# State-space stage of a hybrid decoder step: output products 128 rows wide, the state products of a pair's two groups in turn

## The reference

```python
def s5_mixer(x, ...):
    u = x.reshape(B, L, S5_GROUPS, S5_GROUP)            # 64 groups of 16 channels
    a_re, a_im = mag * cos(li * dt), mag * sin(li * dt)  # 64 complex states a group
    bu_re = einsum('blgc,gpc->blgp', u, bb_re)           # and bu_im
    h = scan(h[t] = a * h[t-1] + bu[t])                  # complex
    y = (einsum('gcp,blgp->blgc', c_re, h_re) - einsum('gcp,blgp->blgc', c_im, h_im)
         + d_skip * u)
    y = gelu(y)
    a, g = split(einsum('bld,de->ble', y, w_glu), 2)
    return a * sigmoid(g), h_re[:, -1], h_im[:, -1]
```

## Time and profile before

| | us |
|---|---|
| median of 3 runs | 1486.23 |
| lowest, highest | 1483.96, 1486.32 |
| span of the profiled execution | 1484.9 |
| PE busy in it | 1419.2 (96%) |
| weight loads (PEld) busy | 1348.5 (91%) |
| DVE busy | 687.8 (46%) |
| ACT busy | 437.6 (29%) |
| POOL busy | 367.2 (25%) |

### The profile page before, as it was taken

One profiled execution on the slowest core, in us unless ns is written; L12 is line 12 of the kernel. 1 busy time (PEld: TensorE's weight loads), 2 busy tenths in 40 slices (PEclk: granted clock), 3 DMA queues, 4 the chain that ended last, 5 costly groups with the idle time before them and its releaser, 6 DMA issues.

```text
span 1484.9 us, 26234 instructions
## 1 busy us (share of the span) xinstructions
PE 1419.2 (96%) x10503; PEld 1348.5 (91%) x10503; DVE 687.8 (46%) x902; ACT 437.6 (29%) x648; POOL 367.2 (25%) x368
## 2 busy tenths in 40 slices
PE   4999999999999999999985999999999999999997
PEld 3999977689999999999984777899999999999997
DVE  6653335656945733434438465134443343332443
ACT  4311143423422413314310011322342341331423
POOL 3010024425999700000376221012200000000032
PEclk9999989999999999999996575699999999999999
DMA  4233221114232223222378131232232222322222
GB/s 136 72 86 85 84 58 39 54 48 104 71 90 81 85 85 85 85 84 77 93 152 104 33 73 41 68 91 76 82 85 84 75 83 85 85 85 85 78 78 79
DMA packets 239142, 119.60 MB, mean 81 GB/s; under 512 B 35512, under 2 KB 235888, under 8 KB 239088
## 3 DMA queue, kind: packets, MB, share of 16 engines
q1 hardware_dynamic: 238832, 118.78, 30.5%
q10 hardware_dynamic: 256, 0.06, 0.0%
HBM read 108.08 MB, written 10.73 MB: 80 GB/s over the span
## 4 chain that ended last, share of the span: by engine, by line
PE 89%; DVE 6%; ACT 1%; issue 1%; SPq 1%; DMA 1%; POOL 0%; DVEq 0%; ACTq 0%; POOLq 0%
PE ps L309 71%; PE ps L1705 5%; PE ps L1703 3%; PE ps L1552 2%; PE ps L1525 2%; DVE wlo L293 1%; PE ps L1684 1%; PE ps L1643 1%; PE ps L1515 1%; PE ps L1561 1%; PE ps L1555 1%; DVE R L330 1%; DMA raw<-in_ffn_w_down 1%; PE ps L1578 0%; PE ps L1764 0%
## 5 line engine op out<-in xcount | busy, mean ns | idle before, releaser
L288 ACT ACTIVATE whi<-raw 128x1024 fp32r<-128x1024 f32 x177 | 187.1, 1057 | 521.9 <-PE ps L309 486.6
L309 PE MATMUL ps<-hid_hi,whi 128*128 128x288 f32 x1408 | 303.1, 296 | 10.4 <-DVE wlo L293 10.4
L309 PE MATMUL ps<-xg_hi,whi 128*128 128x288 f32 x1424 | 306.3, 296 | 3.2 <-DVE wlo L293 1.7
L309 PE MATMUL ps<-xg_hi,wlo 128*128 128x288 f32 x1424 | 304.6, 295 | 0.0
L309 PE MATMUL ps<-xg_lo,whi 128*128 128x288 f32 x1424 | 302.8, 294 | 0.0
L309 PE MATMUL ps<-hid_hi,wlo 128*128 128x288 f32 x1408 | 301.7, 295 | 0.0
L309 PE MATMUL ps<-hid_lo,whi 128*128 128x288 f32 x1408 | 300.6, 295 | 0.0
L293 DVE TENSOR_TENSOR wlo<-raw,whi 128x1024 fp32r<-128x1024 f32 x177 | 247.6, 1399 | 102.6 <-ACT whi L288 102.4
L309 PEld LDWEIGHTS ps<-hid_hi,whi 128*128 128x128 f32 x1408 | 226.4, 189 | 11.4 <-DVE wlo L293 6.3
L309 PEld LDWEIGHTS ps<-xg_hi,whi 128*128 128x128 f32 x1424 | 228.2, 188 | 5.6 <-issue 2.3
L309 PEld LDWEIGHTS ps<-xg_lo,whi 128*128 128x128 f32 x1424 | 228.4, 188 | 0.0
(11 more groups left out here) (347 smaller groups left out, 1260.8 us busy)
## 6 DMA issues: line engine op xcount, KB each, us to landing
raw<-in_ffn_w_up SPq DMA_DIRECT2D x64, 512.0 KB, 4.0
raw<-in_ffn_w_down SPq DMA_DIRECT2D x64, 512.0 KB, 4.0
raw<-in_mlstm_w_in SPq DMA_DIRECT2D x25, 512.0 KB, 3.8
raw<-in_s_w_glu SPq DMA_DIRECT2D x16, 512.0 KB, 3.9
raw<-in_mlstm_w_out SPq DMA_DIRECT2D x8, 512.0 KB, 4.0
MT<-d_taps SPq DMA_DIRECT2D x48, 64.0 KB, 2.5
d_u<-unat SPq DMA_DIRECT2D x8, 288.0 KB, 2.3
U<-d_u SPq DMA_DIRECT2D x16, 144.0 KB, 6.3
```

The costliest lines, as they stand in the source:

```text
L288: nc.scalar.activation(whi[:, s], raw[:, s], ACT.Copy).then_inc(whi_done, 1)
L309: last = nc.tensor.matmul(ps[:, 2 * s + c, 0:HN], w[:, s, k, :], a[:, k, c * HN:(c + 1) * HN], start=(k == 0 and n == 0), stop=(k == KT - ...
```

## The change

The output of a quarter's group is one accumulation of 128 partitions instead of two of 64. For each quarter the taps' products of both groups come first (weights 128 x 128 instead of 128 x 64, twice), then the state products: real part of group 0, of group 1, imaginary part of group 0, of group 1 (weights 64 x 128 instead of 64 x 64). The waits and the last instruction's signal stay.

```diff
                 for q in range(4):
+                    o = [ps[:, 6 + g2, q * COLS:(q + 1) * COLS] for g2 in range(2)]
                     for g2 in range(2):
-                        g8, st = 2 * q + g2, slice(g2 * SP, (g2 + 1) * SP)
-                        for hf in range(2):
-                            o = ps[hf * 64:(hf + 1) * 64, 6 + g2, q * COLS:(q + 1) * COLS]
-                            nc.tensor.matmul(o, taps_of[k][:, g8, hf * 64:(hf + 1) * 64], U2[:, 8 * k + g8, :], start=True, stop=False)
-                            for ri in range(2):
-                                last = nc.tensor.matmul(
-                                    o, CA[st, ri, 4 * k + q, 1 + 4 * hf:5 + 4 * hf, :].rearrange("p j c -> p (j c)"),
-                                    Hst[st, s, ri, q, 0:COLS], start=False, stop=(ri == 1))
+                        nc.tensor.matmul(o[g2], taps_of[k][:, 2 * q + g2, :], U2[:, 8 * k + 2 * q + g2, :], start=True, stop=False)
+                    for ri in range(2):
+                        for g2 in range(2):
+                            st = slice(g2 * SP, (g2 + 1) * SP)
+                            last = nc.tensor.matmul(o[g2], CA[st, ri, 4 * k + q, 1:T + 1, :].rearrange("p j c -> p (j c)"),
+                                                    Hst[st, s, ri, q, 0:COLS], start=False, stop=(ri == 1))
                 last.then_inc(sy_done, 1)
```

## The result

The changed kernel takes a median of 1433.28 us (1429.04 to 1435.41, 4 runs) beside 1486.28 (1483.96 to 1489.10, 4 runs) for the kernel before: ratio 0.963, 95% interval 0.9605 to 0.9654. It is faster and inside the range, by 53 us where 65 were forecast. The profiled execution took 1433.83 us, its span 1431.5.

A forecast was written before the change was run, and what follows sets the result against it. PE's answers were taken as the bound. 69.3 us saved on PE, less 3 of waiting and one in the tail, left 65; the 1484.9 us span became 1419.9, and 1.3 outside it made 1421 us, range 1410 to 1442.

The forecast's parts named there:

- my own case: The prediction's main case for the whole kernel: 1421 us, with its own range 1412 to 1428; chance 0.68.
- sign for paced weights: In the answers' trace: records 0.2 us apart or more would show the forecast wrong, with weights setting the pace.
- What bounds the kernel: In the stage, PE's answers are the bound: eight calls take 120.3 us, 15.04 each, with PE busy throughout.
- New price: A step of the changed answers on PE: 6.4 us at 1.2 GHz, 3.6 at 2.4, middle of the bounds.
- the rival on wide weights: In the answers, 128x128 weights pace records at 0.24 us each at 1.2 GHz: 32 us saved, 1454; chance 0.07.
- The loop after it: PE's 8 answers, 5 gains turns and 6 sums take 72.5 us, all at 1.2 GHz, for 141.8: 69.3 saved.
- What is late next: DVE's states in groups 2 to 4, stretched beside POOL: 3 us of PE waiting, leaving 66.3 saved.
- DVE and POOL become the bound: States of groups 2 to 4 each 5 us longer, two thirds on the path: 10 us, 1431; chance 0.12.
- The tail: After the last answers, tile 7's store waits behind tile 6's fetch: one us counted, leaving 65 saved.
- a passage at every change of row half: In the answers, five passages a quarter in place of two, 9.4 us a step: 45 saved, 1441; chance 0.08.
- Loads in series: In the answers, each record costs load plus matmul, 0.555 us: 62 to 93 us added, 1549 to 1579; chance 0.03.
- The rule against the edit: Skill's up to 2x for outputs of at most 64 columns: old quarter 1.5 us, so widening the answers gains nothing.

The follow-up runs named there:

- e1: Against the changed kernel: 128-column weights kept, but each group's three products (taps, real, imaginary) in series as before the change; 1469.17 us.
- e4: Changed kernel with POOL's gains of steps 5, 6 and 7 left out but for one small operation each; 1417.57 us.
- e6: Changed kernel with POOL's end work waiting for the last states instead of the last sums; 1427.38 us.
- e2: Against the changed kernel: its order of products kept, but with outputs of 64 rows again; 1422.44 us.
- e8: Changed kernel with 64-row outputs, all four quarters' taps before all state products, and POOL's end work behind the last states; 1422.28 us.
- e3: Changed kernel, still wide, with the taps of all four quarters ahead of all state products; 1425.97 us.

## Why the prediction was right, and where it was 12 us off

The direction and the bound were right, and the time lies in the stated range, but not in that of my own case (1412 to 1428): it fell into the room left for the rivals. The prediction's sign for paced weights, records 0.2 us apart or more, came true, and a step took 8.5 us where 5 to 7.5 were to show my case. That the time was still in the range is partly luck, as the terms show.

*What bounds the kernel*: right. The answers were the path through the stage, and their fall from 120.3 to 52.7 us is the gain.

*New price*, 6.4 us a step at 1.2 GHz: **mis-sized**, it is 8.5. The row halves overlap fully, as the lower bound had it, and the passages were about right (0.21 for 0.17). But a record with a 128-column weight takes 0.213 us at 1.2 GHz (16 of them 3.69, two 0.70) and 0.11 at 2.4, not 0.125 and 0.06. That is the mechanism of the rival on wide weights at nearly the price read from the transposes, which I had put down to their 128 streamed columns; they stream 72 here and cost the same. Its time, 1454, was wrong, since it left out the overlap of the halves that the runs show; in series, as it reckoned, e1 gives 1469.

*The loop after it*, all at 1.2 GHz: **wrong in the other direction**. Half of the answers ran at 2.4 GHz, at 4.8 us, so eight took 52.4 us by their starts (52.7 by the windows) where 51.2 were forecast, and gains and sums took 17.4 for 21.3. Two errors cancelled, and that is luck: the price of a step was a quarter too low, the clock taken too slow. The rows were there for the second: before, five of the eight steps ran partly at 2.4 GHz, as their windows of 12.9 to 15.2 us and mean clocks of 0.61 to 0.75 say beside 17.6 us at 0.50.

*What is late next*, 3 us of PE waiting: **this is the step that failed**; it was 15.5, 12.5 more. Less the 2.7 us that PE's loop took under its forecast, the stage is 9.8 us longer than reckoned, most of the miss; 2.3 us more lie outside the stretch up to the weights, in equal code. The slow price beside POOL was right (1.32 us for 0.42), and so was a state of 9 to 11 us beside one gain: step 4 took 9.1. Two things were not seen. A shorter loop delivers its turns sooner, so two gains fell into one state, 14.4 us; and POOL's end work, which stretched the last states before as well, lost its cover. At 2.4 GHz PE's loop is also shorter than the 10.3 us against which I set the states. e4 and e6 show both by taking POOL's work out of the states: 11.1 and 3.9 us of waiting go. The rival "DVE and POOL become the bound", at 1431, describes what happened better than my case.

*The tail*, +1 us: **the number was right, by luck, and its reason wrong**. Nothing held the store of tile 7 behind the fetch of tile 6: with PE's wait of 5.41 us before the last answers, tile 6's fetch was out by 899.99 us, the store followed ACT's copy at once, and the fetch came 5.9 us behind the last answers, not about 7. The 0.7 us came from PE's product, which ran 1.8 us longer at the slow clock. What was forecast came about in e2: there ACT's copy of the last tile is done at 888.45 us, and its store starts at 891.32, right behind the fetch of tile 6 at 890.94.

*Of the rivals*, a passage at every change of row half falls: eight state records by turns take 1.06 us, with one passage. Loads in series falls: the stage got shorter, at 0.213 us a record. (The lower end of its sum, 1549, is 1548 by its own terms.)

*The rule against the edit* deserves a second look. By the Trainium skill (TensorEngine Tiling, Theoretical Speedup and Key Properties) small tiles run side by side, and a change of tiling mode drains the engine. The trace of the changed kernel alone could not weigh it; e2 does: with the passages thinned out, four small tiles run at once, and a quarter takes 1.37 us, under the 2.12 of the wide one and close to the 1.5 that the prediction worked out for the old records side by side. By that rule widening gains nothing; measured, it costs 11 us of the stage (85.3 against 74.4).

## What to carry to other kernels

When a change alters two things, shape and order, price each alone: here the order made the gain and the shape took part of it back. When a bound is cut in two, list what the engines behind it did under its cover, with their slowest prices, and ask which of their works now fall together. And before one engine's work is put off to speed up another, look for who reads its result: POOL's end work, put off, became the next wait (3.5 us in e8).

## What was new of the hardware

- A 128-column f32 weight sets 0.213 us a record at 1.2 GHz and 0.11 at 2.4, with 72 columns streamed as with the 128 of the transposes. The Trainium skill (TensorE: Matmul & The Clock Gate, LDWEIGHTS) gives columns / 1.2 ns for a weight load and names no clock with it, an estimate of 107 ns for 128: the spacing of the records agrees at 2.4 GHz, and is twice that at 1.2. That it is the load which sets the pace is argued from the shapes, not shown by itself. The load rows leave it open: at 1.2 GHz a load of 128 columns lasts 0.32 us on average in the answers of the changed kernel, one of 64 columns 0.21 before, but one of 128 columns in the transposes 0.22.
- Records in both row halves of the array start together (eight in the time of four), and 64 x 64 pieces four at once.
- A passage between weights of different shapes costs 0.21 us at 1.2 GHz with 128 columns (e3), 0.17 with 64.
- After PE had idled 7.54 and 5.41 us, the next answers ran at a granted clock of 0.50 (1.2 GHz); the four steps at 1.00 (2.4 GHz) followed sums directly or, once, a pause of 0.41 us; the one behind a pause of 2.17 us began at 2.4 GHz and fell. Before, answers of 13 to 15 us also began at 2.4 GHz, or reached it within 1 us, and fell midway with PE busy throughout; four steps of 4.8 us were over without a fall. Why it rises and falls where it does stays open; no run was made for it.
